# Second triangular solve begun before head 1 is placed, a weight split moved, row sums on 32-row outputs, and final_g applied on ScalarE

## The reference, cut to what matters

```python
def swiglu(u, w_in, w_out):
    gate, up = jnp.split(u @ w_in, 2, axis=-1)
    return (jax.nn.silu(gate) * up) @ w_out
...
ml = (jax.nn.silu(c) @ w_ada[li] + b_ada[li]).reshape(B, N_MOD, D)            # modulation of the latents
mc = (jax.nn.silu(c_ctx)[None] @ w_ada[li] + b_ada[li]).reshape(1, N_MOD, D)  # and of the context
...
# chunked gated delta rule, per head, direction and chunk (the kernel uses chunks of 128 tokens)
sol = lax.linalg.triangular_solve(eye + a_low, rhs, left_side=True, lower=True, unit_diagonal=True)
...
return rmsnorm(h, final_g)      # h * rsqrt(mean(h*h) + EPS) * final_g
```

## Time and profile before

| | |
|---|---|
| median of 3 runs | 2952.06 us (2951.28 to 2956.73) |
| the profiled execution | 2957.31 us, of which the span of the trace is 2955.5 us |
| PE busy (matmuls) | 2880.7 us, 97% of the span |
| PE busy (weight loads) | 2521.3 us, 85% |
| DVE / ACT / POOL busy | 1683.2 / 963.9 / 235.9 us (57% / 33% / 8%) |
| memory traffic | 541.62 MB, 183 GB/s on average |
| granted TensorE clock | 0.988 of full speed |

### The profile page before, as it was taken

The page is one execution under the profiler, slowest core; times in us unless marked ns, Lnnn a source line. Parts: engine busy times, 40 slices in busy tenths (PEclk is TensorE's granted clock), DMA queues, the critical chain, the costliest instruction groups (busy, mean ns, idle before and its releaser), DMA issues. The chain is left out here.

```text
span 2955.5 us, 47731 instructions
## 1 busy us (share of the span) xinstructions
PE 2880.7 (97%) x18176; PEld 2521.3 (85%) x18176; DVE 1683.2 (57%) x2469; ACT 963.9 (33%) x1434; POOL 235.9 (8%) x390
## 2 busy tenths in 40 slices
PE   6999999999999999999999999998999999999998
PEld 3677888888888888888887888878999999999998
DVE  2522547465575757475637566755675555555555
ACT  2211222222221222222224455543354444433443
POOL 3000000000000000000002013545120000000001
PEclk9999999999999999999999999999999999999999
DMA  9765245545455757667533466684556666566564
GB/s 360 288 209 168 93 144 158 166 145 173 140 170 164 263 178 247 205 211 239 175 91 84 134 188 191 195 268 154 160 160 187 188 186 186 180 185 185 185 191 134
DMA packets 399049, 541.62 MB, mean 183 GB/s; under 512 B 51024, under 2 KB 301904, under 8 KB 390240
## 3 DMA queue, kind: packets, MB, share of 16 engines
q1 hardware_dynamic: 377264, 434.20, 47.4%
q10 hardware_dynamic: 21680, 106.03, 11.0%
HBM read 518.08 MB, written 22.05 MB: 183 GB/s over the span
## 5 line engine op out<-in xcount | busy, mean ns | idle before, releaser
L1650 DVE TENSOR_TENSOR wl<-raw,wh 128x1024 fp32r<-128x1024 f32 x640 | 782.6, 1232 | 761.0 <-ACT wh L1297 759.3
L1297 ACT CAST wh<-raw 128x1024 fp32r<-128x1024 f32 x640 | 665.9, 1047 | 1538.2 <-PE ps L714 1165.8
L712 PE MATMUL ps<-xh,wh 128*128 128x512 f32 (+1 forms) x1920 | 733.8, 382 | 7.1 <-issue 4.6
L713 PE MATMUL ps<-xl,wh 128*128 128x512 f32 (+1 forms) x1920 | 724.2, 377 | 0.0
L714 PE MATMUL ps<-xh,wl 128*128 128x512 f32 (+1 forms) x1920 | 723.4, 377 | 0.0
L712 PE MATMUL ps<-hth,wh 128*128 128x512 f32 (+1 forms) x1408 | 470.5, 334 | 0.9 <-DVE wl L1650 0.9
L714 PE MATMUL ps<-hth,wl 128*128 128x512 f32 (+1 forms) x1408 | 471.0, 334 | 0.0
L713 PE MATMUL ps<-htl,wh 128*128 128x512 f32 (+1 forms) x1408 | 470.3, 334 | 0.0
L712 PEld LDWEIGHTS ps<-xh,wh 128*128 128x128 f32 x1920 | 363.4, 189 | 78.2 <-issue 9.4
L714 PEld LDWEIGHTS ps<-xh,wl 128*128 128x128 f32 x1920 | 362.6, 189 | 68.2
L713 PEld LDWEIGHTS ps<-xl,wh 128*128 128x128 f32 x1920 | 363.5, 189 | 64.8
(11 more groups left out here) (246 smaller groups left out, 2333.4 us busy)
## 6 DMA issues: line engine op xcount, KB each, us to landing
raw<-in_ffn_w_in SPq DMA_DIRECT2D x704, 256.0 KB, 3.2
raw<-in_ffn_w_out SPq DMA_DIRECT2D x176, 512.0 KB, 4.2
abuf<-in_w_ada ACTq DMA_DIRECT2D x64, 1024.0 KB, 5.5
ada_t<-in_ada SPq DMA_DIRECT2D x64, 512.0 KB, 9.1
abuf<-in_w_ada ACTq DMA_DIRECT2D x64, 512.0 KB, 3.7
raw<-in_w_in SPq DMA_DIRECT2D x128, 256.0 KB, 3.5
gate_t<-in_ada SPq DMA_DIRECT2D x32, 512.0 KB, 5.0
raw<-in_w_out SPq DMA_DIRECT2D x32, 512.0 KB, 4.3
```

Of the source, the lines that this page charges most:

```text
L712: mm(out, ah, bh, start=first, stop=False)
L713: mm(out, ah, bl, start=False, stop=False)
L1297: nc.scalar.copy(wh[:, t % HL, :], raw[:, t % RAW, :]).then_inc(hi_done, 1)
L1650: tt(wl[:, t % HL, :], raw[:, t % RAW, :], wh[:, t % HL, :].bitcast(F32), ALU.subtract).then_inc(lo_done, 1)
```

## The change

Five edits, each on its own:

- POOL: `lanes(1, 0)` runs ahead of `place(1)` and `lanes(1, 1)` right behind it; the third part follows the placing of head 2. The cuts go from (13, 26) to (8, 19) steps.
- SP: `level_blocks(4)` stands ahead of `set_load(3)`, and `lane_store(1)` moves from head 2 to the end of head 1's loads.
- ACT and DVE: the split of tile T_WOUT + 2 moves from ahead of the scan into `scan(0)`, behind the first `vn` copies on ACT and behind `negate_tn32(1)` on DVE.
- Row sums: 16 matmuls with 128x128 weights give way to 4 with 32 columns of ones as weights and 512 columns of `acc` moving, each into its own 32 partitions of bank 7 (`reduce_rows`, behind tile 1); DVE copies the whole bank to SBUF (`reduced_rows`, at j = 2); 4 matmuls with 128x128 blocks of that copy as weights and 4 moving columns turn the rows into columns (`reduce_columns`, behind tile 3).
- End: ACT scales all 16 blocks by final_g inside the last group, four behind each four squares; DVE multiplies them by the factor straight out of PSUM in five operations of 4, 4, 4, 2 and 2 blocks; POOL has no part; five transfers.

```diff
-LANE_STEPS = (((0, 11), (11, 21), (21, BLK - 1)), ((0, 13), (13, 26), (26, BLK - 1)))
+LANE_STEPS = (((0, 11), (11, 21), (21, BLK - 1)), ((0, 8), (8, 19), (19, BLK - 1)))
...
@@ sync
-                last = h in (0, 2)
-                if h + 2 < HEADS and not last:
+                if h and h + 2 < HEADS:
                     level_blocks(h + 2)
                 if h + 1 < HEADS:
                     set_load(h + 1)
-                if h == 2:
+                if h == 0:
+                    level_blocks(2)
+                if h + 2 < HEADS:
+                    level_rows(h + 2)
+                if h == 1:
                     lane_store(1)
-                if h + 2 < HEADS:
-                    if last:
-                        level_blocks(h + 2)
-                    level_rows(h + 2)
...
@@ tensor
+            def reduce_rows():
+                for c_ in range(4):
+                    s, half = divmod(c_, 2)
+                    i = mm(ps[32 * c_:32 * (c_ + 1), 7, :], ones.broadcast_to([P, 32]),
+                           acc[:, s, half * TILE_N:(half + 1) * TILE_N], start=True, stop=True)
+                i.then_inc(red_pe, 1)
+
+            def reduce_columns():
+                for b in range(4):
+                    i = mm(ps[:, 7, b:16:4], rsum[:, b * P:(b + 1) * P], sel4, start=True, stop=True)
+                i.then_inc(red_pe, 1)
...
-                        if reduced and p == 0 and 1 <= k <= 4:
-                            if k == 1:
-                                pe.wait_ge(acc_done, steps(r, s - 1, KT))
-                                pe.wait_ge(gated[f], gates(f, r, s - 1, 4))
-                            i = reduce(k - 1)
-                            if k == 4:
-                                i.then_inc(red_pe, 1)
+                        if reduced and p == 0 and k == 1:
+                            pe.wait_ge(acc_done, steps(r, s - 1, KT))
+                            pe.wait_ge(gated[f], gates(f, r, s - 1, 4))
+                            reduce_rows()
+                        elif reduced and p == 0 and k == 3:
+                            pe.wait_ge(red_out, r * 2 + (2 * (s - PIECE_FROM) - 1))
+                            reduce_columns()
...
@@ scalar
+            def last_blocks(b):
+                squares(3, 1, 1, range(4 * b, 4 * b + 4))
+                for k in range(4 * b, 4 * b + 4):
+                    fn(h_ctx[:, k, :], h_lat[:, k, :], ACT.Copy, scale=cols[:, C_FG + k:C_FG + k + 1]
+                       ).then_inc(fin_scaled, 1)
...
                 copies(0)
                 if h:
                     out_squares(h - 1)
+                else:
+                    split(0, 0, T_WOUT + AHEAD - 1)
...
@@ vector
+            def reduced_rows(r, s):
+                dve.wait_ge(red_pe, r * 2 + (2 * (s - PIECE_FROM) - 1))
+                V.tensor_copy(rsum[:], ps[:, 7, :]).then_inc(red_out, 1)
...
-            V.tensor_copy(rb, ps[:, 5, 0:SEQ]).then_inc(rb_set, 1)
-            dve.wait_ge(rb_set, 1)
-            for k in range(FIN_POOL, KT):
-                stt(h_ctx[:, k, :], h_lat[:, k, :], cols[:, C_FG + k:C_FG + k + 1], rb,
-                    ALU.mult, ALU.mult).then_inc(fin_done, 1)
+            dve.wait_ge(fin_scaled, KT)
+            for i, n in enumerate(FIN):
+                k = slice(sum(FIN[:i]), sum(FIN[:i + 1]))
+                tt(h_ctx[:, k, :], h_ctx[:, k, :], bc(ps[:, 5, 0:SEQ], n), ALU.mult).then_inc(fin_done, 1)
...
@@ gpsimd
             place(0)
+            lanes(1, 0)
             place(1)
-            lanes(1, 0)
+            lanes(1, 1)
             for h in range(1, HEADS):
                 if h + 1 < HEADS:
                     place(h + 1)
                 out_power(h - 1)
-                if h < len(LANE_STEPS[1]):
-                    lanes(1, h)
+                if h == 1:
+                    lanes(1, 2)
```

More of the change, by code:

```diff
@@ L64 @@
 GROUP_TILES = UP_TILES + N_OUT * OUT_TILES
-FIN_POOL = 5
+FIN = (4, 4, 4, 2, 2)
 PIECE_FROM = 2
@@ L147 @@
 C_SEL = C_FG + KT
-C_ONE = C_SEL + 2
+C_SEL4 = C_SEL + 2
+C_ONE = C_SEL4 + 4
 C_POSR = C_ONE + 1
@@ L176, in host_constants @@
     pools = np.stack(pools, axis=1)
-    sel = np.concatenate([i % 32 == s for s in range(2)], axis=1)
+    sel = np.concatenate([i % 32 == s for s in range(2)] + [i == 32 * c for c in range(4)], axis=1)
     tail = np.concatenate([sel, np.ones((P, 1)), waves(SEQ // GRID_W), waves(GRID_W), ident], axis=1)
@@ L276, in build @@
         sel = cols[:, C_SEL:C_SEL + 2]
+        sel4 = cols[:, C_SEL4:C_SEL4 + 4]
         cols_c = cols[:, C_CONV:C_CONV + 105]
@@ L699, in _ @@
                 group_loads(1, g, 0, T_FFN2)
-            for k, n, made in ((5, 4, fin_done), (0, 5, fin_pool), (9, 4, fin_done), (13, 3, fin_done)):
-                sp.wait_ge(made, n if made is fin_pool else k + n - FIN_POOL)
+            for i, n in enumerate(FIN):
+                k = sum(FIN[:i])
+                sp.wait_ge(fin_done, i + 1)
                 sp.dma_start(out[:, k:k + n, :], h_ctx[:, k:k + n, :]).then_inc(out_done, 16)
-            sp.wait_ge(out_done, 16 * 4)
+            sp.wait_ge(out_done, 16 * len(FIN))
         @block.tensor
@@ L1603, in _ @@
             for k in range(K_TILES):
-                split(0, 0, T_POOL + K_TILES + k + AHEAD)
+                if k < K_TILES - 1:
+                    split(0, 0, T_POOL + K_TILES + k + AHEAD)
                 if k == 2:
@@ L1633, in _ @@
                 group(1, r, 1, T_FFN2 + GROUP_TILES)
-            group(1, 0, LAST, T_FFN2 + LAST * GROUP_TILES, closing=lambda b: squares(3, 1, 1, range(4 * b, 4 * b + 4)))
-            for k in range(FIN_POOL):
-                fn(h_ctx[:, k, :], h_lat[:, k, :], ACT.Copy, scale=cols[:, C_FG + k:C_FG + k + 1]
-                   ).then_inc(fin_scaled, 1)
+            group(1, 0, LAST, T_FFN2 + LAST * GROUP_TILES, closing=last_blocks)
         @block.vector
@@ L1805, in group @@
                         split(r, GROUP_TILES, base + j + AHEAD)
+                    if j == 2 and evac:
+                        reduced_rows(r, s)
                     if j == 5 and evac:
@@ L2324, in _ @@
             norm(3, SEQ)
-            pool.wait_ge(fin_scaled, FIN_POOL)
-            pool.wait_ge(rb_set, 1)
-            for k in range(FIN_POOL):
-                tt(h_ctx[:, k, :], h_ctx[:, k, :], rb, ALU.mult).then_inc(fin_pool, 1)
 _INS = ["x", "c", "ctx", "c_ctx", "w_ada", "b_ada", "norm_g", "w_in", "conv_w", "a_log", "dt_bias",
```

13 lines of the change are left out of this document (6 added, 7 removed).

## The result

The changed kernel takes 2934.34 us (median of 6 runs, 2931.49 to 2938.92), the kernel before beside it 2952.70 us (6 runs, 2951.28 to 2956.73): ratio 0.9932, 95% interval 0.9923 to 0.9942. Forecast were 2932.6 us, in a range from 2925 to 2944. The profiled execution took 2935.78 us, span 2934.0 us.

What follows compares the result with a forecast made beforehand. PE, busy nearly all the time, was taken to bound the kernel. Row sums -12.6, scan -8.3 and end +1.4 sum to -19.5 us, taking 2952.1 to 2932.6 us, range 2925 to 2944.

Steps and rivals of the forecast that it cites:

- Row sums: First FFN's reductions: 3.80 us of PE removed, 0.95 and 1.27 added, 1.58 us gained eight times, -12.6 us.
- Head 3: Scan: the 5.1 us wait for `FI` and 2.8 us of lower-clock matmuls behind it go, -7.9 us.
- Head 2: Scan: the 1.1 us wait and 1.7 us lost to the lower clock behind it go, -2.8 us.
- Head 0's join: Scan: POOL finishes eight substitution steps before placing head 1, so this join comes 2.4 us later.
- The moved split: Scan's opening: its gain, PE's 3.77 us wait for `vn`, is eaten by the wait for head 1's placing.
- The end: Last group and output: norm factor 3.7 us later, DVE's operations behind it 2.3 us shorter, net +1.4 us.
- the scan's order: POOL's substitution and placing, heads 0 to 3: 2.4 - 7.9 - 2.8 = -8.3 us, ends -11 and -3.
- the row sums one after another: Rival, first FFN: four row sums take 3.78 us, +7.4 us in all, 2952.6 us, no change; chance 0.05.
- with bare loads: Rival, first FFN: serial row sums also wait for weight loads, 5.3 us, +19.6 in all, 2964.8 us; chance 0.03.
- the substitution without gain: Rival, scan: POOL slower beside DVE or head 0 loses more, scan only -3 us, 2937.9 us; chance 0.08.
- The lower clock at the end: Rival, last products: two new waits bring the clock to 1.2 GHz, costing 2.8 us, 2935.4 us; chance 0.28.
- The four row sums fully together: Rival, first FFN: four row sums cost one matmul, 0.95 us, gain 15.2 us, 2930.0 us; chance 0.12.

Runs made afterwards that it cites:

- rows_only: The kernel before with only the row sums of the change: 2940.84 us, ratio 0.9956 to the kernel before.
- rows_serial: The changed kernel with all four row sums written to one group of partitions, 0 to 31: 2954.91 us, ratio 1.0010 to the kernel before.
- order_only: The kernel before with only POOL's and SP's new order and the new cuts, split still ahead of the scan: 2948.45 us, ratio 0.9981.
- split_back: The changed kernel with the split of tile T_WOUT + 2 put back ahead of the scan: 2933.14 us, ratio 0.9929 to the kernel before.
- after_again: The changed kernel run once more, unchanged: 2934.01 us, ratio 0.9935 to the kernel before.
- final_only: The kernel before with only the new end, final_g on ACT and five DVE operations: 2956.49 us, ratio 1.0008.
- place_first: The changed kernel with head 1 placed before the second substitution, which then runs 18 and 13 steps: 2931.47 us, ratio 0.9931 to the kernel before.
- four_parts: The changed kernel with ACT's scalings in idle time, substitution cut into 2, 13, 12 and 4 steps, XP behind head 1's output power: 2930.16 us, ratio 0.9926.
- place_14: The changed kernel with head 1 placed before the second substitution, which then runs 14 and 17 steps: 2936.81 us, ratio 0.9939 to the kernel before.

## Why the prediction was right, and where it was not

- **Row sums**, forecast -12.6: the stage shows -13.1, `rows_only` -13.0. The row block was 1.22 us for 1.27 forecast from the gate columns, the column block 0.95 as the old piece. `rows_serial` shows that the choice between the two bounds, 1.27 and 3.78, carried the whole forecast: the other end was measured as 3.77. The working misreads rows 4 in one point, where it says that they do not follow the page's rule fully. They do: the first eight of that block's sixteen records take 0.64 us (PE's timeline up to 153.2 us), and the remainder of the 1.27 is two more such rounds and the way into the block and out of it.

```profile
152.80 0.64 PE L720 MATMUL ps<-gate_t,cpad 128*32 128x256 f32 x8
```

- **Head 3**, forecast -7.9: 25.89 became 17.96. **Head 2**, -2.8: it was -2.5. But both were read against one execution: head 3 took 1.6 and 2.3 us less in two other runs of the old order, and head 2 was as short as 19.5 in one of them. Hence `order_only` gained 5.4 us, and not the 10.7 that these two terms promise: against 92.6 and 92.0 us its 86.4 for heads 0 to 3 is 6 less, against the 95.7 of the profile before 9 less.
- **Head 0's join**, forecast +2.4: it was mis-sized; head 0 stayed at 25.0 us (-0.1), and the four profiles of this order have 25.0 to 26.6 where three with the old order and the unmoved split have 23.8 to 25.1. The step that failed is the time at which head 1 is placed, 8.6 us after the token tiles' end by the forecast's sum, 6.8 in the trace (1963.9 against 1957.1). LT was in place 1.1 us earlier than said (POOL starts at 1948.35); the clearing and eight steps took 9.0 us instead of 11.7; the placing took 6.5 instead of 4.6. The last two have one cause, below. PE's wait was 2.3 us, not "about 5", though 4.6 and 4.3 in two other runs; what sets it apart from run to run stays open.
- **The moved split**: "it also eats what the moved split gives" is right; `split_back` shows no gain from the split beyond the scatter of head 0.
- **The end**, forecast +1.4: the stage shows +1.2, but 0.8 of that lie ahead of the last group. The end itself is +0.4 in the profile and +0.8 in `after_again` and `final_only`. Counted from the cast of tile 19 the factor came 3.2 us later (3.7 forecast). PE's waits, 1.29 and 2.06 us, were shorter than the 1.6 and some 2.6 said, so step n = 3 started 2.7 us later and not 3.4; the third batch held the factor back by 0.5 and not 0.3. Behind the norm step 2.4 to 2.8 us were saved (2.3 forecast): DVE's five operations took 4.68 us instead of 4.9. `final_only` gives +2.6 by its median, with the interval reaching to 0.
- **Scale**: the profiled pair differs by 21.5 us, the medians by 18.4; the forecast of 19.5 lies between. In the scan the execution before spent more time at the low clock than others of its kind, 27 us against 24 and 17, and the forecast's working took that for the rule. So the closeness of the sum is in part luck: the scan's order, with -8.3 forecast, gave -5.4 alone, and the end cost less than said. The mechanisms of the row sums, of the waits in heads 2 and 3 and of the two waits at the end came as described.

Of the rivals, the row sums one after another (and with bare loads), and the substitution without gain, did not come. The lower clock at the end did not come in this profile, where the granted clock is 1.00 from 2905 to 2925, although the rival's time, 2935.4, is nearer to the result than the forecast's 2932.6. In `place_first`, which has the same end, it did come, for 3.4 us:

```profile
2910.70:2914.10 3.40, 3.40 (x19) 3.40 (x17) 0.90 (x3) 2.54 (x7) 2.57 (x4) 0.50 0.01 2
```

It cost 1.0 us there (28.5 from the cast to the norm step, for 27.5), less than the 2.8 that the rival put on it. The four row sums fully together is what happened, 1.06 us for four and 1.04 for one; only the rival's price was wrong, 0.95 us per block, since a quarter of the serial block shares out by four what each block pays once. It measured 1.22.

## What to carry to other kernels

Where TensorE is the bound, it pays to write narrow matmuls into different groups of 32 output partitions: four took the time of one here, and with the way into the block and out of it cost 3.1 times less than four in one group, which gained nothing over the old form. Keep such matmuls in one block, since each block paid about 0.33 us once. When an in-order helper engine has no gap left (POOL in the changed kernel), do not stop at curing the wait that shows: list the due time of each of its results, since each cured wait came back at the next one here. Price a stall from several executions, since the low clock at much the same wait lasted 3 to 10 us, and put work with slack behind, never ahead of, what the bounding engine waits for.

## What the runs showed of the hardware

**A POOL operation can stand still while a DVE operation runs.** POOL's copies take 0.28 us; two of head 1's took 1.28 and 1.31:

```profile
1957.65 1.28 POOL L2276 COPY GI<-CP 32x128 f32<-32x128 f32 x1
1958.97 0.28 POOL L2276 COPY GI<-CX 32x128 f32<-32x128 f32 x1
1959.21 1.31 POOL L2276 COPY GI<-CP 32x128 f32<-32x128 f32 x1
```

and DVE's timeline has a weight split over each of them:

```profile
1957.43 1.35 DVE L1668 TENSOR_TENSOR wl<-raw,wh 128x1024 fp32r<-128x1024 f32 x1 [9.97 <-ACT wh L1308]
...
1959.16 1.21 DVE L1668 TENSOR_TENSOR wl<-raw,wh 128x1024 fp32r<-128x1024 f32 x1
```

Between 1935 and 2130 us the traces of before, after and `place_first` have 18 copies and substitution steps of POOL that are 0.7 to 1.0 us longer than their neighbours of the same kind, and each of them met a weight split of DVE (two inputs from SBUF); of the more than 500 operations that met none, none is long. Which of the two began first decides. Each of the 18 began 0.05 to 0.43 us behind the start of a split and ended 0.15 to 0.45 us behind its end. Of the 38 others that met a split, 23 began first or in the same instant and kept their length, 7 began in its last 0.1 to 0.3 us and lost at most that, and 8 are additions of squares, each of which ends 0.60 us behind the split that it met. The Trainium skill (SBUF — State Buffer, "Who interferes with whom") says that the two engines share a port pair as an exclusive lock, that a DVE instruction with two SBUF inputs contends with a GpSimd instruction that reads SBUF, and that the order of issue decides who blocks; the trace agrees. This is the cause of both mis-sized durations: in the kernel before three splits lengthened operations of the eight steps (11.7 us), in the changed one none did (9.0), and two fell into the placing. It works the other way too, as far as one row can say it: in `four_parts` DVE's two short operations on `o` took 2.25 us (0.48 in the changed kernel) beside POOL's copy of XP, from 2003.03 to 2004.97.

**The clock.** The granted clock stood at 1.2 GHz for 17 us in head 0, from the end of the wait of 2.21 us on and through that of 2.34, and for 10 us in `place_first`, beginning 0.4 us before the end of a single wait of 2.61. In `place_14` it fell for 6.8 us in head 0 though no wait of PE there was over 0.8 us. Behind 1.29 and 2.06 us, 8 us apart at the end, it did not fall in six profiles, and fell for 3.4 us in `place_first`, with the same two waits. What tells these cases apart was not tried and stays open.
